# Head norms four at a time, a start in half units, and small reorderings in a two-layer kernel bound by TensorE

## The reference

```python
q = rms_norm(q.reshape(b, s, 8, 128), q_norm_w)
k = rms_norm(k.reshape(b, s, 8, 128), k_norm_w)
s = where(k_pos <= q_pos, (q @ k.T) * 128 ** -0.5, -inf)   # causal, one block of 256
attn = softmax(s) @ v
```

## Time and profile before

| | |
|---|---|
| three runs | 1561.07, 1561.35, 1567.77 us (median 1561.35) |
| profiled execution, its own time | 1567.55 us |
| span of the profiled execution | 1565.9 us |
| TensorE busy | 1542.4 us (99%) |
| VectorE, ScalarE busy | 1156.0 us (74%), 787.9 us (50%) |
| mean granted TensorE clock | 0.994 |

### The profile page before, as it was taken

The page is one execution under the profiler, slowest core; times in us unless marked ns, Lnnn a source line. Parts: engine busy times, 40 slices in busy tenths (PEclk is TensorE's granted clock), DMA queues, the critical chain, the costliest instruction groups (busy, mean ns, idle before and its releaser), DMA issues. The chain is left out here.

```text
span 1565.9 us, 33333 instructions
## 1 busy us (share of the span) xinstructions
PE 1542.4 (99%) x13186; PEld 1524.3 (97%) x13186; DVE 1156.0 (74%) x1370; ACT 787.9 (50%) x960; POOL 29.7 (2%) x56
## 2 busy tenths in 40 slices
PE   9999998999999999999999999999899999999997
PEld 8999997999999999999999999999899999999997
DVE  7777798658898878888788887888854644764754
ACT  7545545645554444444444444444554644454543
POOL 0000000000000000000000000000000000000000
PEclk9999999999999999999999999999999999999999
DMA  9474555448787767677676776765365554445441
GB/s 339 157 269 162 194 170 176 161 164 279 259 294 268 270 235 286 234 261 270 233 287 232 264 269 233 289 231 200 133 242 189 189 186 151 161 158 181 162 159 71
DMA packets 85361, 339.31 MB, mean 217 GB/s; under 512 B 9488, under 2 KB 9760, under 8 KB 78752
## 3 DMA queue, kind: packets, MB, share of 16 engines
q1 hardware_dynamic: 77328, 281.05, 52.1%
q0 software_dynamic: 7232, 54.55, 9.8%
q10 hardware_dynamic: 720, 2.53, 0.4%
HBM read 335.97 MB, written 2.12 MB: 216 GB/s over the span
## 5 line engine op out<-in xcount | busy, mean ns | idle before, releaser
L1260 PE MATMUL PS<-gh,whi 128*128 128x256 f32 x3504 | 985.6, 281 | 2.9 <-DVE gl L1144 1.7
L1262 PE MATMUL PS<-gl,whi 128*128 128x256 f32 x3504 | 974.2, 278 | 0.0
L1264 PE MATMUL PS<-gh,wlo 128*128 128x256 f32 x3504 | 973.9, 278 | 0.0
L658 DVE TENSOR_TENSOR wlo<-raw,whi 128x1024 fp32r<-128x1024 f32 x528 | 642.7, 1222 | 348.7 <-ACT whi L296 346.2
L296 ACT ACTIVATE whi<-raw 128x1024 fp32r<-128x1024 f32 x528 | 556.5, 1059 | 642.9 <-PE PS L1264 640.1
L1260 PEld LDWEIGHTS PS<-gh,whi 128*128 128x128 f32 x3504 | 660.9, 189 | 8.6 <-issue 5.2
L1262 PEld LDWEIGHTS PS<-gl,whi 128*128 128x128 f32 x3504 | 662.2, 189 | 2.6 <-issue 1.9
L1264 PEld LDWEIGHTS PS<-gh,wlo 128*128 128x128 f32 x3504 | 660.3, 188 | 0.0
L1260 PE MATMUL PS<-ah,whi 128*128 128x256 f32 x688 | 190.1, 276 | 0.9 <-DVE al L1028 0.9
L1264 PE MATMUL PS<-ah,wlo 128*128 128x256 f32 x688 | 189.9, 276 | 0.0
L1262 PE MATMUL PS<-al,whi 128*128 128x256 f32 x688 | 189.9, 276 | 0.0
(11 more groups left out here) (228 smaller groups left out, 787.8 us busy)
## 6 DMA issues: line engine op xcount, KB each, us to landing
raw<-weights SPq DMA_DIRECT2D x528, 512.0 KB, 3.7
ada_w<-w_ada POOLq DMA_DIRECT2D x48, 1024.0 KB, 6.5
EM<-rows POOLq DMA_DIRECT2D x1, 3072.0 KB, 11.8
outT<-X SPq DMA_DIRECT2D x4, 512.0 KB, 3.0
X<-xT SPq DMA_DIRECT2D x3, 512.0 KB, 8.2
c<-const ACTq DMA_DIRECT2D x1, 1536.0 KB, 7.0
c_act<-c_rows POOLq DMA_DIRECT2D x1, 1024.0 KB, 6.5
X<-xT SPq DMA_DIRECT2D x2, 256.0 KB, 4.8
```

What stands on the lines that cost most here:

```text
L658: dve.tensor_tensor(wlo[:, j % SPLIT, :], raw[:, j, :], whi[:, j % SPLIT, :].bitcast(F32), ALU.subtract).then_inc(s_lo, 1)
L1260: pe.matmul(out[:, t, :], whi[:, b, w], hi[:, kt, :], start=first and half == 0 and (apart or t % 2 == 0), stop=False, skip_group_check=True)
L1262: pe.matmul(out[:, t, :], whi[:, b, w], lo[:, kt, :], start=False, stop=False, skip_group_check=True)
L1264: mm = pe.matmul(out[:, t, :], wlo[:, b, w], hi[:, kt, :], start=False, stop=last and half == 1, skip_group_check=True)
```

## The change

Head norms: four heads at once, with NORMS = (62, 74). Each head's sums go to 32 partitions of one tile (`ones[:, 0:32]`), so one root and one reciprocal do for four heads of q and k. k is multiplied by its factor, which PE spreads over the partitions, and by both norm weights; q's factor is transposed to columns and goes into the scores' scaling on DVE. In slots 78 and later a new order on PE has the transposes first, and then halves of the scores and of the weighted sum in turn.

```diff
-NORMS = (58, 61, 64, 67, 74, 75, 76, 77)
+NORMS = (62, 74)
+GAINS = (15, 17, 18, 19, 20, 21, 22, 23, 25, 26, 27, 28)
+FINAL = ((4, 1), (5, 1), (6, 2), (8, 2), (10, 2))
+HALVED = 2
 # ACT: squares at NORMS[b] - 2 and - 1 (four heads of q, then of k), root at NORMS[b]
+                    if n - NORMS[b] in (-2, -1):
+                        head_squares(b, n - NORMS[b] + 2)
 # DVE
+            def head_inverse(b):            # slot NORMS[b] + 1
+                dve.wait_ge(s_nrt, b + 1)
+                dve.reciprocal(HRT[:, :, :], HRT[:, :, :]).then_inc(s_inv, 1)
+            def k_norm(h):                  # slots NORMS[b] + 3 and + 4, two heads in each
+                dve.scalar_tensor_tensor(t, t, qk_norm, PS[:, 5 + h % 4 // 2, S * (h % 2):S * (h % 2) + S],
+                                         ALU.mult, ALU.mult).then_inc(s_qk, 1)
+                        for c, at in enumerate((slice(0, P), slice(P, 3 * P))):
+                            ins = dve.scalar_tensor_tensor(seen(h, c), PS[:, 4, at], q_col(h, c), mask[:, at],
+                                                           ALU.mult, ALU.add)
 # PE
+                        for h in range(4):
+                            mm = pe.matmul(PS[32 * h:32 * h + 32, 7, :], ones[:, 0:32], HSQ[:, h, :, :], ...)
+                    if n == NORMS[b] + 3:
+                        pe.wait_ge(s_inv, b + 1)
+                        for c in range(2):
+                            mm = pe.transpose(PS[:, 7, P * c:P * c + P], HRT[:, 0, P * c:P * c + P], ident)
...
+                        for h in range(4):
+                            mm = pe.matmul(PS[:, 5 + h // 2, S * (h % 2):S * (h % 2) + S],
+                                           ident[:, 32 * h:32 * h + 1].to_broadcast([P, P]), HRT[:, 1, :], ...)
+            def weighted(h, layer, PTS, VS, parts):     # now keys 128 to 255 first, then 0 to 127
```

```diff
+                if j < HALVED:
+                    sp.dma_start(raw[:, j, 0:512], weights[j, :, 0:512]).then_inc(s_half[j], 16)
+                    sp.dma_start(raw[:, j, 512:], weights[j, :, 512:]).then_inc(s_raw[j], 16)
 # ACT and DVE, in the loop over the eight units u of the first group
-                if u < 4:
+                if u < HALVED:
...
+                else:
                     split(B_IN, u)
             for n in range(IN_SLOTS):
-                split(B_IN, LEAD + n)
+                if n >= DT // 2 - LEAD:
+                    split(B_IN, LEAD + n)
 # PE
-            for _ in range(13):
+            for _ in range(8):
-                if n == 6:
+                if n == 7:
                     pe.wait_ge(s_cst, 16)
                     sum_squares(0, SQX1)
```

The dt steps of slots 15, 17 and 18 are now in 14 and 16, their transposes on PE at 20 instead of 21, and `c_act`'s SiLU at 67 instead of 78. In layer 2 and around it:

```diff
+            def idle(n):
+                for _ in range(n):
+                    pe.matmul(PS[:, 4, 0:S], ident, cst[:, 0:S], start=True, stop=True)
 # PE: after column_squares(2); in the first feed-forward round ahead of down(0); in slot 2 of layer 2
+                if k == 2:
+                    idle(2)
+                if i is first:
+                    pe.wait_ge(s_root, 2)
+                    idle(2)
+                if n == 2:
+                    idle(2)
 # PE, first unit of layer 2: whi by gh, wlo by gh, and only then whi by gl
+                    for w, x in ((whi, gh), (wlo, gh), (whi, gl)):
+                        if x is gl:
+                            pe.wait_ge(s_gl, need(kt))
 # PE, column_squares: order of the tiles
+                order = (1, 2, 3, None) if k == 2 else (None, 2, 3)
 # DVE, last round of the feed-forward part and after it
-                    if i is last and j == 6:
-                        ffn_lo(i, ah2, al2)
                     if j % 2:
                         add_to_x(unit + (16 + j), grp + (2 + j // 2), (G_FF + j // 2) % 2, 4 * (j // 2))
+                    if i is last and j == 5:
+                        ffn_lo(i, ah2, al2)
             last_add(2)
+            last_add(3)
             dve.wait_ge(s_fold, 3)
 # output of layer 2, ACT
-                if s in (13, 15, 23, 31):
+                if s in (14, 16, 24, 31):
...
+                if s in GAINS:
+                    t = GAINS.index(s)
+                    gained(t, SQUARES[3] + t // 4 + 1)
 # DVE: sum_chunk at s = 16 and 24 instead of 15 and 23
 # the end, DVE: six pieces instead of three ahead of the last tile; seven DMAs out instead of four
-            for first, tiles in ((4, 4), (8, 4), (12, 3)):
+            for first, tiles in FINAL + ((12, 3),):
```

More of the change, by code:

```diff
@@ L302, in squares @@
             def squares(k, c, buf):
+                if k == 3 and c == 2:
+                    act.activation(small[:, 241:242], col("eps"), ACT.Sqrt).then_inc(s_warm, 1)
                 if k == 2 and c == 3:
@@ L1250, in _, with product @@
         def _(pe):
-            def product(b, out, tiles, first, last, hi, lo, apart=False, ready=None):
+            def product(b, out, tiles, first, last, hi, lo, apart=False, ready=None, halved=None):
                 for half in range(2):
@@ L1257, in product @@
                         pe.wait_ge(s_gl, ready(kt))
+                    if halved is not None:
+                        pe.wait_ge(s_lo if half else s_lohalf, halved + 1)
                     for t in range(4):
@@ L1358, in attention @@
                 if step == 0:
[L1359 to L1368 removed]
+                    scores(h, layer, q, k, range(2))
                 if step == 4:
@@ L1404, in attention, with scores @@
-                    mm.then_inc(s_pv, 1)
+                    weighted(h, layer, PTS, VS, (1, 0))
+            def scores(h, layer, q, k, parts):
+                H = layer * HEADS + h
+                for c in parts:
+                    if c == 0:
+                        if layer:
+                            pe.wait_ge(s_evac, (G_IN2 + 10 if h < 4 else G_IN2 + 13) + 2)
+                        else:
+                            pe.wait_ge(s_qk, h + 1)
+                        if H >= 1:
+                            pe.wait_ge(s_sb, H)
+                    at, keys = (S * c, S) if layer else (P * c, P + P * c)
+                    mm = pe.matmul(PS[:, 4, at:at + keys], q[:, P * c:P * c + P], k[:, 0:keys], start=True, stop=True)
+                    if c == 1:
+                        mm.then_inc(s_sc, 1)
@@ new lines, in weighted @@
+            def weighted(h, layer, PTS, VS, parts):
+                H = layer * HEADS + h
+                for b in parts:
+                    if b == 1:
+                        pe.wait_ge(s_pts, H + 1)
+                        pe.wait_ge(s_vs, H + 1)
+                        if layer and h:
+                            pe.wait_ge(s_gated, h)
+                        if not layer and h:
+                            pe.wait_ge(s_ahi, h)
+                            if h > 4:
+                                pe.wait_ge(s_gl, DT + 6 + h - 4)
+                    first = 0 if layer else P * b
+                    mm = pe.matmul(PS[:, 6, first:S], VS[:, h % 2, b, :], PTS[:, h % 2, b, 0:S - first],
+                                   start=(b == 1), stop=(b == 0), skip_group_check=True)
+                    if b == 0:
+                        mm.then_inc(s_pv, 1)
@@ new lines, in first_heads, with head @@
+            def first_heads(n):
+                def head(step):
+                    h, odd = divmod(n - ATT0 - step, 2)
+                    return h if not odd and 0 <= h < HEADS else None
+                new, mid, old = head(0), head(4), head(6)
+                if mid is not None:
+                    attention(4, mid, 0)
+                for part in range(2):
+                    if new is not None:
+                        scores(new, 0, QKVZ[:, head_tile(Q0, Q1, new), :], QKVZ[:, head_tile(K0, K1, new), :], (part,))
+                    if old is not None:
+                        weighted(old, 0, PTS1, VS1, (1 - part,))
@@ L1488, in _ @@
+                first_heads(n)
             W1, W3 = DTW[:, 1, :], DTW[:, 3, :]
```

252 lines of the change are left out of this document (142 added, 110 removed).

## The result

The changed kernel took 1582.9 us (median of 4; 1582.07 to 1584.55) beside 1561.2 us for the kernel before. The ratio is 1.014 [1.012, 1.016]: slower by 22 us, where 12 us of gain were forecast. The forecast was wrong, and its time is outside the range. What happened is the rival B, to which I had given 0.06, and the rival C beside it. The ratios in this text leave out single executions that took over 1.5% more than the fastest of their kernel; the medians have them in.

What follows compares the result with a forecast made beforehand. PE bounds the kernel, busy 1542.4 of 1565.9 us, through its gaps and pace. Terms sum to -11.65 us, -17.75 with the 57 units' pitch: 1567.55 to 1549.8 us; own range 1546.5 to 1553, widened to 1546 to 1557.5.

Steps and rivals of the forecast that it cites:

- rival B: Idle matmuls in the first feed-forward round draw the slow pitch behind them: 24.7 us, 1574.5 us; chance 0.06.
- rival C: Pauses of 2.4 and 0.8 us at the start pull the clock down: up to 3.4 us, 1553.2 us; chance 0.09.
- part 4: Feed-forward: `al` ready before PE comes, -1.0 us; two idle matmuls in the first round, +0.9 us.
- Part 1: Start: ACT's order delays the squares, so PE pauses for the sum before unit 8: +1.45 us net.
- Part 2: dt: steps end three slots earlier in DVE's order, so PE's wait for DTW goes: -0.9 us.
- Part 3: Head norms: wait at first scores and low clock go, with new small waits, -6.5 us; pitch, -0.5 us.
- Part 5: Into layer 2: earlier squares on PE and earlier gl, no low clock; -2.5 us up to its ninth unit.
- Part 7: Output of layer 2: one gain per slot removes the wait for wlo and the slow pitch: -2.0 us.
- Part 8: End: first output piece ready 0.8 us sooner, limited by seven issues replacing four: -0.6 us.
- Part 6: 57 units of layer 2 at the quick pitch: -6.1 us against the profiled execution, nothing against the median.
- Rival A: 57 units of layer 2 run at the slow pitch in most runs: 1555.9 us; chance 0.26.

Runs made afterwards that it cites:

- experiment 7: Changed kernel with the two idle matmuls of the first feed-forward round writing different halves of the PSUM bank; 1580.2 us, 1.010.
- experiment 9: Changed kernel with the two feed-forward idle matmuls given different weights, columns and PSUM halves; 1576.2 us, 1.008.
- experiment 11: Changed kernel without feed-forward idle matmuls, with one in slot 2 and the start's conversions and splits in the order of before; 1548.5 us, 0.991.
- experiment 12: As experiment 11, with NORMS = (61, 74) instead of (62, 74); 1553.5 us, 0.994.
- experiment 3: Changed kernel without the idle matmuls in the feed-forward round and without those in slot 2 of layer 2; 1556.3 us, 0.996.
- experiment 6: Changed kernel with four idle matmuls instead of two in the first feed-forward round; 1583.8 us, 1.015.
- experiment 8: Changed kernel with the two feed-forward idle matmuls cut to 128 columns; 1583.1 us, 1.015.
- experiment 5: Changed kernel with three idle matmuls instead of two in the first feed-forward round; 1557.2 us, 0.997.

## Why the prediction was wrong

**The failed step** is in part 4: "Two idle matmuls in the first round cost two times 0.43 us, in the open", with what was said against rival B, "in the trace a bare 256- or 512-column interruption from the quick pitch, without a wait, left it quick each time". That cost was right (0.68 us and 0.19 behind it, 0.87 in all). What failed is that the term held nothing for the pitch behind the pair: what the pair did to the 5568 matmuls there is worth 24.8 us; rival B had 24.7. Experiment 1 takes the pair away and gets the 25 us back, experiment 2 adds it to the kernel before and loses them.

The sentence against B was true, and yet it held no precedent for this pair. The trace of before has 19 interruptions by 256- or 512-column matmuls alone from the quick pitch without a wait: 12 by a single matmul, 6 by two (scores, or attention times V, in layer 2) and one by five, and the pitch stayed quick behind all of them. None was a pair of idle matmuls, and the sentence took them for one kind with it. The number of matmuls does not tell them apart either, since two score matmuls are two as well. The trace of before also had interruptions that turned the pitch each time: four matmuls with weights of 64 columns between products, two over 256 columns and two over 128, eight instructions. Their timeline (which shows the form of the first), and windows of 5 us ahead of and behind each:

```profile
125.97 0.87 PE L1468 MATMUL PS<-EM,XD 128*64 128x256 f32 x8
132.62 0.87 PE L1468 MATMUL PS<-EM,XD 128*64 128x256 f32 x8
```

```profile
120.00:125.00 5.00, 5.00 (x47) 1.00 0.49 147
127.00:132.00 5.00, 5.00 (x44) 1.00 0.67 199
134.00:139.00 5.00, 5.00 (x46) 1.00 0.56 198
140.20:145.20 5.00, 5.00 (x45) 1.00 0.58 184
```

The counts are 47, 44, 46, 45, with two or three cut by the edges in each: 113.3 to 113.7 ns and 117.8 ns in turn. Over the traces of all fourteen kernels, 84 such groups without a wait changed the pitch 84 times, 55 from quick to slow and 29 back. The 32 instructions of the dt product (L1420, L1539) did so 14 times in 14, and the four of DTW's transposes (L1430, L1549), where they came without a wait, 12 times in 12. I had seen that pitches change at interruptions, had written that an inserted matmul is a new draw, and then priced the draw by neighbours of another kind. A term of 24.7 us that hung on one event had a chance of 0.06 by them. What makes an idle pair unlike two score matmuls, the experiments don't show.

**Part 1, the start: size too small.** Forecast: unit 8 at 34.5 us, the folds' end at 33.3, 2.4 us of pause. Measured 34.73, 33.45, and 1.67 + 0.47 us of waits. The pause was sized about right, +1.5 us net; what is missing is the clock behind it:

```profile
31.64 0.28 PE L1326 MATMUL PS<-gh,wlo 128*128 128x256 f32 x1
33.60 0.67 PE L1434 MATMUL PS<-SQX,cst 128*128 128x256 f32 x2 [1.67 <-DVE SQX L723]
34.73 0.36 PE L1322 MATMUL PS<-gh,whi 128*128 128x256 f32 x1 [0.47 <-DVE wlo L688]
```

ACT's order was the reason, as worked out: the squares begin at 24.31 us (forecast 24.1).

```profile
17.98 1.06 ACT L316 ACTIVATE whi<-raw 128x1024 fp32r<-128x1024 f32 x1 [1.46 <-DMA raw<-weights]
...
24.31 2.00 ACT L331 ACTIVATE SQX<-X 128x1024 f32<-128x1024 f32 x2
```

But rival C came as well: the clock was 0.50 (1.2 GHz) from 35.4 to 38.8 us. Unit 10 began at 43.84 us, 3.2 later than before, where 1.45 was forecast. The argument against C, that the pauses which had pulled the clock down were longer, didn't hold: the clock fell behind 1.67 us without work, one matmul and 0.47 us more. It is not a rule, though. Of the ten profiled kernels with this start eight show a clock of 0.50 behind waits of 2.0 to 3.0 us in all. The kernels of experiments 7 and 9 show 1.00 throughout behind 2.4 and 2.8 us, and their unit 10 begins at 42.33 us. The row and the window of experiment 7:

```profile
33.51 0.67 PE L1434 MATMUL PS<-SQX,cst 128*128 128x256 f32 x2 [1.98 <-DVE SQX L723]
```

```profile
35.00:45.00 10.00, 10.00 (x102) 1.00 0.73 236
```

In experiments 11 and 12, where PE doesn't wait for the sum, the clock there stayed at 1.00.

**Part 2, dt:** from unit 10 to 24 the changed kernel won 0.6 us, forecast 0.9. The wait for DTW went, and one of 0.6 us for `small` (L1555) came two steps further on.

**Part 3, the head norms: right.** Between unit 24 and unit 120 it won 6.6 us (2.6 behind, then 4.0 ahead), forecast 6.5 and 0.5. The wait at the first scores and the low clock behind it are gone, and no wait for `al` is left in part 4 either (-1.2, forecast -1.0). The new waits were to be 1.4 and 0.2 us:

```profile
218.02 0.44 PE L1608 MATMUL PS<-cst,HRT 128*128 128x128 f32 x2 [1.43 <-DVE HRT L896]
```

and 0.29 for the other (1.7 in all). The 0.5 us of pitch did not come: in the new order from slot 78 on most stretches ran at 117.8 ns.

**Parts 5, 7 and 8: right in sum.** Forecast -5.1, measured -5.0. Part 5 gave -2.5, as forecast: the gap of PE between the feed-forward part and layer 2 is 5.5 us (1131.2 to 1136.7) instead of 7.2, and the first eight units took 0.8 us less. The clock fell there all the same, against the forecast, but for 3.4 us instead of 6.8, so that the number is right in part by luck. How long it falls is not settled by the kernel: of the twelve profiled kernels with this passage nine show 3.4 us, two 6.8 us and that of experiment 3 none. Part 7 gave -2.2 (forecast -2.0): the wait for `wlo` is gone, and the output runs at 113.3 ns where the slow pitch stood. Part 8 gave -0.3 (forecast -0.6): from DVE's first multiplication to the last instruction it takes 7.8 us, before 8.2.

**Part 6, the 57 units: forecast -6.1, measured 0 in the profiled execution.** The pair in slot 2 drew the slow pitch, in the changed kernel and in experiment 1. Five profiled executions have the quick pitch ahead of that pair (these two, and experiments 6, 7 and 9), and all five are slow behind it. The times of experiments 1 and 3 have two levels some 6 us apart, which I read as both pitches; experiment 3's profiled one, at 1551.3 us, has the quick one. Rival A was the better forecast for these units, in about half of the executions and more. The argument against it came from runs of a kernel without this pair.

The difference of 33.2 us between forecast (1549.8) and profiled execution (1582.95) is thus 24.8 of the feed-forward pitch, 6.1 of the 57 units, 1.75 of the start, and terms of half a microsecond and less. With one matmul in place of the pair, experiment 4 came near the forecast in its median, 1551.3 us; its five executions lie between 1549.0 and 1560.3, by the draws that are left, so part of that nearness is luck. The forecast against the median, 1561.35 - 11.55, has a slip of 0.1: the sum is -11.65.

## What to carry to other kernels

Before pricing an edit of a stream bound by TensorE, divide each long window by its instructions; if there are two paces at one granted clock, every matmul put between the products is priced by what stands behind it, 4.45 ns times thousands, not by its own 0.3 us. A precedent from the trace counts only if it has the same matmuls; like columns or a like number are not enough. Where there is none, run the kernel with and without the insertion, several executions each. An order in which one engine makes its inputs evenly is no gain if it delays the chain that feeds a later sum: here it cost a pause of 2 us and, in eight of ten traces, about 1.5 us more behind it with the low clock.

## What the runs showed of the hardware

The same product matmuls of 256 columns (operands in fp32r) run at 113.3 or 117.8 ns at a granted clock of 1.00, for 650 us on end, and a pair of unrelated matmuls ahead of them can decide which. The Trainium skill, page "TensorE: Matmul & The Clock Gate", section "Back-to-back issue gap", gives the 109 ns that the prediction worked with as the gap of an isolated matmul; for a stream of weight loads and matmuls it has figures for 128 and 512 columns (about 81 and 131 ns), and none for 256. No run here showed 109 ns in the products. From the quick pitch, with no wait, in place of the pair: one or three left it quick (14 of 14 executions), two or four made it slow (27 of 30, counting the changed kernel's four and experiment 2). Both counts go by the times. From the slow pitch a pair did not always switch back: in slot 2 it left the slow pitch slow in experiments 4 and 8 and made it quick in experiment 5.

It is not a rule of odd and even for all matmuls: two score matmuls (L1487) in layer 2 left the quick pitch quick in every trace, 56 times, and so did two of attention times V (L1505), 28 times in layer 2 and 14 times at the end of layer 1. Why these differ from an idle pair is open, as is what the two paces are physically. Open too is why four of the 55 executions of the kernels without a pair or a four in the feed-forward part took 1576.1 to 1579.6 us. Of the 65 executions of the kernel before, which has no idle matmul there, three took 1584.5 to 1587.6 us, some 25 us more than the usual 1561. That is the price of the slow pitch in the feed-forward part, so it may be drawn without a pair as well, though rarely. None of these seven was profiled, so it is not shown.
